# Gated stages of width 2816: three of four sums of weight blocks per pack by adding transfers, into doubled buffers

## The reference

```
def _swiglu(x, w_gate, w_up, w_down):
    return (jax.nn.silu(x @ w_gate) * (x @ w_up)) @ w_down
```

## Time and profile before

| | |
|---|---|
| time, median of 2 runs | 3442.8 us (3442.07 to 3443.53) |
| profiled execution, span from first to last instruction | 3441.6 us |
| TensorE busy | 3396.0 us, 99% of the span |
| VectorE busy | 2436.4 us, 71% |
| ScalarE busy | 1659.5 us, 48% |
| GpSimd busy | 133.9 us, 4% |
| TensorE clock granted, mean | 0.998 |
| DMA | 91 GB/s, 27% of the 16 engines' time in the SP queue |

### The profile page before, as it was taken

How to read it: one execution, slowest core, us unless ns; L and a number is a source line. 1 busy time by engine, 2 the same in 40 slices (tenths; PEclk the granted TensorE clock), 3 DMA queues, 4 the chain that set the end, 5 groups by cost and what they waited for, 6 DMA issues and landing times. The chain is left out here.

```text
span 3441.6 us, 63684 instructions
## 1 busy us (share of the span) xinstructions
PE 3396.0 (99%) x24351; PEld 3124.3 (91%) x24351; DVE 2436.4 (71%) x3572; ACT 1659.5 (48%) x2508; POOL 133.9 (4%) x129
## 2 busy tenths in 40 slices
PE   9999999999999999999999999999999999999998
PEld 8998899989998987887899889999999998799987
DVE  6886878877888655655888865657785367867863
ACT  4553655545554433333455545546555344455552
POOL 0100202000200100000002000000000000000000
PEclk9999999999999999999999999999999999999999
DMA  4333223332333322222223331212223321022232
GB/s 142 108 110 111 87 86 110 105 116 86 105 109 111 104 74 80 74 80 74 74 98 110 116 99 62 68 61 68 99 98 98 98 69 50 32 74 95 96 104 80
DMA packets 89618, 311.58 MB, mean 91 GB/s; under 512 B 10800, under 2 KB 15280, under 8 KB 89296
## 3 DMA queue, kind: packets, MB, share of 16 engines
q1 hardware_dynamic: 89056, 307.19, 26.9%
q0 software_dynamic: 368, 1.68, 0.2%
HBM read 306.73 MB, written 2.10 MB: 90 GB/s over the span
## 5 line engine op out<-in xcount | busy, mean ns | idle before, releaser
L821 PE MATMUL ps<-x_hi,w_hi 128*128 128x264 f32 (+2 forms) x2176 | 707.5, 325 | 2.6 <-ACT pair L2593 0.9
L821 PE MATMUL ps<-x_hi,w_lo 128*128 128x264 f32 (+2 forms) x2176 | 695.9, 320 | 0.0
L821 PE MATMUL ps<-x_lo,w_hi 128*128 128x264 f32 (+2 forms) x2176 | 694.1, 319 | 0.0
L2698 DVE TENSOR_TENSOR w_lo<-raw,w_hi 128x1024 fp32r<-128x1024 f32 x277 | 337.4, 1227 | 299.2 <-ACT w_hi L1685 296.8
L821 PEld LDWEIGHTS ps<-x_hi,w_hi 128*128 128x128 f32 x2176 | 410.1, 188 | 54.0 <-issue 17.8
L821 PEld LDWEIGHTS ps<-x_lo,w_hi 128*128 128x128 f32 x2176 | 409.6, 188 | 30.3
L821 PEld LDWEIGHTS ps<-x_hi,w_lo 128*128 128x128 f32 x2176 | 410.9, 189 | 28.6
L821 PE MATMUL ps<-h_hi,w_hi 128*128 128x264 f32 (+3 forms) x1296 | 410.7, 317 | 5.3 <-DVE h_lo L2905 1.9
L821 PE MATMUL ps<-h_hi,w_lo 128*128 128x264 f32 (+3 forms) x1296 | 399.6, 308 | 0.0
L821 PE MATMUL ps<-h_lo,w_hi 128*128 128x264 f32 (+3 forms) x1296 | 398.8, 308 | 0.0
L1685 ACT ACTIVATE w_hi<-raw 128x1024 fp32r<-128x1024 f32 x277 | 289.3, 1055 | 74.7 <-PE ps L821 50.6
(11 more groups left out here) (378 smaller groups left out, 7669.3 us busy)
## 6 DMA issues: line engine op xcount, KB each, us to landing
raw<-wstream SPq DMA_DIRECT2D x577, 512.0 KB, 3.3
res<-xT SPq DMA_DIRECT2D x8, 256.0 KB, 7.3
out<-res SPq DMA_DIRECT2D x8, 256.0 KB, 2.2
bias<-consts POOLq DMA_DIRECT2D x1, 1024.0 KB, 5.4
g_chunk<-consts POOLq DMA_DIRECT2D x1, 264.0 KB, 3.2
g_keep<-consts POOLq DMA_DIRECT2D x1, 256.0 KB, 3.3
par<-params SPq DMA_DIRECT2D x1, 232.5 KB, 7.7
ident<-consts SPq DMA_DIRECT2D x1, 64.0 KB, 6.4
```

The source lines that it names most:

```text
L821: m = pe.matmul(ps[:, bank, 0:n], w[:, slot, wt, :], x[:, k, c0:c0 + n], start=first and q == 0, stop=last and q == 2)
L2698: dve.tensor_tensor(w_lo[:, slot], raw[:, slot], w_hi[:, slot].bitcast(F32), ALU.subtract)\
```

## The change

The first three sums of a pack are no longer made on VectorE. GpSimd issues seven transfers of 256 KB per pack instead, each from the weights in HBM (`wstream`): three plain copies of B1 into three sum blocks, then two transfers that add B2 into two of them (`accum_op=ALU.add`), then two that add A1, to one of these and to the third block. The second kind waits for all three copies to have landed (M["copy"]), the third for the second (M["mid"]); the last two raise M["acc"]. VectorE keeps the fourth sum (`sum_4`), which waits for M["acc"], and ACT's step 1 waits for M["acc"] too. The sums of every second pack go to a second buffer, `m_sum1`, laid into columns of `x_hi` and `x_lo` (channels of the first half, tokens of the second half) that the packs don't read; its rows of 512 bytes are spaced by 528 floats. The transfers of pack m begin once the low parts of pack m - 2 are made (M["lo"] 2m - 2); those of the first pack of a stage wait for M["t"], those of the second for the end of the plain units (s_unit), which read the same columns of x. The scaling of `res` is moved: one instruction of 128x256 between the packs' transfers, from the third pack of a stage on, 16 in a stage.

```
+        m_sum1 = at("m_sum1", [P, 2, KD, T], offset=x_hi_at)
...
+        def made_block(up, s, b):
+
+            if up % 2:
+                return m_sum1[:, s, 0:KH, META + HALF + P * b:META + HALF + P * b + P]
+            return m_sum[:, 2 * s + b]
+
+        def made_pair(up, s):
+
+            if up % 2:
+                return m_sum1[:, s, 0:KH, META + HALF:T].rearrange("p k (b n) -> p b k n", b=2)
+            return m_sum[:, 2 * s:2 * s + 2]
+
+        def by_block(ap):
+
+            return ap.rearrange("p (b k) n -> p b k n", b=2)
...
                     if step in (0, 3):
                         load_of(u + step // 2 % 2, pack_slot(st, 2 * up + (step == 3)))
+                    elif step == 1:
+                        act.wait_ge(M["acc"], 32 * m + 32)
                     else:
-                        act.wait_ge(M["sum"], 3 * m + 3 - (step == 1))
+                        act.wait_ge(M["sum"], m + 1)
                     if first:
                         act.wait_ge(s_unit, st["u0"] + 4 + step + 1)
...
                     else:
-                        x = m_sum[:, 2:4] if step == 1 else m_sum[:, 0:2]
-                        act.activation(w_hi[:, slot], x.rearrange("p b k n -> p (b k) n"), ACT.Copy).then_inc(M["hi"], 1)
+                        act.activation(by_block(w_hi[:, slot]), made_pair(up, step % 2), ACT.Copy).then_inc(M["hi"], 1)
...
-                def sums_13(i, up):
+                def sum_4(i, up):
 
                     i, up = after(i, up)
-                    u = st["u0"] + 4 * i + 2 * up
-                    s = pack_slot(st, 2 * up)
-                    load_of(u, s)
-                    load_of(u + 1, s + 1)
-                    past(dve, M["lo"], 2 * pack_of(st, i, up))
-                    dve.tensor_tensor(made[:, 0:4:3], blocks[:, 2 * s:2 * s + 4:3],
-                                      blocks[:, 2 * s + 2:2 * s + 3].to_broadcast([P, 2, KH * P]), ALU.add)\
-                        .then_inc(M["sum"], 1)
-
-                def sum_2(i, up):
-
-                    i, up = after(i, up)
-                    m = pack_of(st, i, up)
-                    dve.wait_ge(M["sum"], 3 * m + 1)
-                    dve.tensor_tensor(made[:, 2], made[:, 3], blocks[:, 2 * pack_slot(st, 2 * up)], ALU.add)\
-                        .then_inc(M["sum"], 1)
-
-                def sum_4(i, up):
-
-                    i, up = after(i, up)
-                    m = pack_of(st, i, up)
-                    dve.wait_ge(M["sum"], 3 * m + 2)
-                    dve.tensor_tensor(made[:, 1], made[:, 2], blocks[:, 2 * pack_slot(st, 2 * up) + 1], ALU.add)\
-                        .then_inc(M["sum"], 1)
+                    m, u = pack_of(st, i, up), st["u0"] + 4 * i + 2 * up
+                    load_of(u, pack_slot(st, 2 * up))
+                    dve.wait_ge(M["acc"], 32 * m + 32)
+                    dve.tensor_tensor(made_block(up, 0, 1), made_block(up, 1, 0), raw[:, pack_slot(st, 2 * up), KH:KD],
+                                      ALU.add).then_inc(M["sum"], 1)
...
                 def packs(i, parts=(0, 1)):
                     for up in parts:
                         p, q, r = pack_banks(up)
-                        sums_13(i, up + 1)
+                        sum_4(i, up + 1)
                         add(i, up, 2, 1, r, 0, 0)
-                        sum_2(i, up + 1)
-                        sum_4(i, up + 1)
                         low(i, up + 1, 0)
                         add(i, up, 5, 3, p, 1, 1)
                         low(i, up + 1, 1)
...
+            def weight_sums(st, i, up):
+
+                m, u = pack_of(st, i, up), st["u0"] + 4 * i + 2 * up
+
+                def block(unit, half):
+                    return wstream[unit, :, KH * half:KH * half + KH]
+
+                if i == 2:
+                    pool.wait_ge(M["t"], 4 * st["r0"] + 4)
+                    if up:
+                        pool.wait_ge(s_unit, st["u0"] + 8)
+                else:
+                    pool.wait_ge(M["lo"], 2 * m - 2)
+                for b in range(2):
+                    pool.dma_start(made_block(up, 1, b), block(u + 1, 0)).then_inc(M["copy"], 16)
+                pool.dma_start(made_block(up, 0, 0), block(u + 1, 0)).then_inc(M["copy"], 16)
+                pool.wait_ge(M["copy"], 48 * m + 48)
+                for b in range(2):
+                    pool.dma_start(made_block(up, 1, b), block(u + 1, 1), accum_op=ALU.add).then_inc(M["mid"], 16)
+                pool.wait_ge(M["mid"], 32 * m + 32)
+                for b in range(2):
+                    pool.dma_start(made_block(up, b, 0), block(u, 0), accum_op=ALU.add).then_inc(M["acc"], 16)
+
+            def packs(st):
+
+                done = s_res if before(st)["kind"] == "load" else s_scale
+                for i in range(2, KF // 2):
+                    for up in range(2):
+                        weight_sums(st, i, up)
+                        if i > 2:
+                            r = res[:, i - 3, half_cols(S, up)]
+                            pool.tensor_scalar(r, r, ALPHA, None, ALU.mult).then_inc(done, 1)
+
...
                 b = before(st)
-                if st["kind"] == "glu":
-                    pool.wait_ge(M["t"], 4 * st["r0"] + 4)
-                    pool.wait_ge(M["mul"], 3 * quad_of(st, 5))
-                if b["kind"] == "load":
-                    for k in range(KD):
-                        pool.wait_ge(s_xlo, KD + k + 1)
-                        pool.tensor_scalar(res[:, k, META:T], res[:, k, META:T], ALPHA, None, ALU.mult)\
-                            .then_inc(s_res, 1)
-                    return
...
-                if n and (before(st)["kind"] == "load" or before(st).get("scaled")):
+                if st["kind"] == "glu":
+                    packs(st)
+                elif n and before(st).get("scaled"):
                     scale_residual(st)
```

More of the change, by code:

```diff
@@ L505, in build @@
         M = {name: sem("s_m_" + name) for name in (
-            "t", "thi", "tlo", "sum", "hi", "lo", "prod", "snap", "add", "silu", "mul")}
+            "t", "thi", "tlo", "copy", "mid", "acc", "sum", "hi", "lo", "prod", "snap", "add", "silu", "mul")}
         W = {name: sem("s_w_" + name) for name in (
@@ L1964, in project @@
                 if not st["n0"]:
-                    act.wait_ge(s_res, KD)
+                    act.wait_ge(s_res, 2 * KD)
                     act.wait_ge(s_eps, 1)
@@ L2723, in glu @@
                 last = KF // 2 - 1
-                blocks = raw[:, :, :, :].rearrange("p s (b k) n -> p (s b) (k n)", b=2)
-                made = m_sum[:, :, :, :].rearrange("p b k n -> p b (k n)")
                 def combine(c):
@@ L2809, in low @@
                         return
-                    x = m_sum[:, 2:4] if step == 1 else m_sum[:, 0:2]
-                    dve.tensor_tensor(w_lo[:, slot], x.rearrange("p b k n -> p (b k) n"), w_hi[:, slot].bitcast(F32),
+                    dve.tensor_tensor(by_block(w_lo[:, slot]), made_pair(up, step % 2), by_block(w_hi[:, slot]).bitcast(F32),
                                       ALU.subtract).then_inc(s_lo if step == 1 else M["lo"], 1)
@@ L2922, in glu @@
                 combined_low(3)
-                sums_13(2, 0)
-                sum_2(2, 0)
                 sum_4(2, 0)
@@ L3081, in project @@
                 if not st["n0"]:
-                    dve.wait_ge(s_res, KD)
+                    dve.wait_ge(s_res, 2 * KD)
                 else:
```

## The result

The changed kernel takes 4011.03 us (median of 2 runs, 4006.78 to 4015.27) against 3442.8 (3442.07 to 3443.53): ratio 1.165 [1.162, 1.168]. The direction and the mechanism came as forecast, but it cost 568 us where 188 were forecast, and the time lies above the range. The profiled execution has a span of 4012.9 us.

A forecast was written before the change was run, and what follows sets the result against it. TensorE was taken to bound the kernel (9.91 us per pack), then GpSimd's round. Per stage 9.6 + 1.3 + 2.4 + 33.6 = 46.9 us, four stages 188, giving 3631 us; range 3464 to 3880.

The forecast's parts named there:

- GpSimd's round sets the period: Packs 4 to 17 of each stage: GpSimd's 12.3 us against TensorE's 9.9, 2.4 us lost each, 33.6 per stage.
- R: GpSimd's own round per pack, without the last wave's landing: 12.3 us, 11.2 without a scaling, against TensorE's 9.91.
- wave of copies: First wave, GpSimd's three plain copies: 0.56 x 2 + 3.3 + 0.3 = 4.7 us until landed.
- second wave: Two transfers adding B2, taken as twice a copy's traffic: 2.8 us behind a fixed 2.6, 5.4 us.
- third wave, issue: GpSimd's issuing of the last two adding transfers, whose landing it doesn't wait for: 1.1 us.
- rival 1: Packs: chain hidden but for each stage's start, 3464 us, or 3502 with adding transfers as cheap as copies; chance 0.17.
- rival 2: Packs: adding transfers land after 7.3 us, each such wave 7.9, round 14.8, chain 20.5, 3811 us; chance 0.32 with worse.
- Pack 1's term: Its chain starts only with pack 0, so TensorE's product 7 of pack 0 comes at 18.1 instead of 8.5: 9.6 us lost.
- The engines' load: DMA engines per pack: 3.1 us of SP's loads plus 7.7 of the seven transfers, 10.8 us in a 9.91 us period.
- L: Latency of a pack's whole chain of three waves: 4.7 + 5.4 + 5.4 = 15.5 us.
- crowded row: Profile row of 256 KB transfers in a crowd at the program's start, 7.3 us, taken as an adding transfer's upper price.
- Rival 3: Stage starts: stalls lower TensorE's clock, four 10 us stalls adding 7 us; left in the range, no chance given.

The follow-up runs named there:

- experiment 1: Changed kernel with the four adding transfers of each pack made plain copies, same number, size, order and waits: 3718.9 us.
- experiment 6: Changed kernel with the scaling of res issued behind the stage's last transfers instead of between the packs: 3960.7 us.
- experiment 9: Changed kernel cut to two copies and two adding transfers per pack, VectorE making all sums of packs 0 and 1: 3522.56 us, ratio 1.023 to the kernel before.
- experiment 10: Changed kernel cut to one copy and one adding transfer per pack from pack 2 on, VectorE making all other sums: 3442.31 us, ratio 1.000.
- experiment 11: Separate program without the reference's work, only groups of transfers into both layouts, each waited for: two adding into whole rows 6.1 us, three copies 5.0 us.
- experiment 8: Changed kernel with GpSimd also waiting for the third wave to land before it scales and issues the next pack's copies: 4234.7 us.

## Why the prediction was wrong in size

**The model held.** "GpSimd's round sets the period": a wait-free succession of rounds, and experiments 1, 6, 9 and 10 move the time as the round does, down to no loss where it fits. From the landing to product 7 the prediction counted 2.6 us: 2.6. TensorE's loss is at product 7, VectorE's idle time is before sum 4 with a DMA as its releaser, the first packs are a term of their own, and the removed additions were worth 0 (experiment 10: 41 us of VectorE gone, ratio 1.000).

**The step that failed is the sizing of two waves in R.** For even packs, whose sums have whole rows (in brackets the odd ones, with rows of 512 bytes):

| term | predicted | measured |
|---|---|---|
| "wave of copies" | 4.7 | 7.3 (7.7) |
| "second wave" | 5.4 | 7.5 (8.7) |
| third wave, issue | 1.1 | 1.1 (1.5) |
| scaling | 1.1 | 0.8 |
| R | 12.3 | 16.8 (18.8), mean |

- *4.7 for the copies* left out that the third wave of the pack before is still in flight. The prediction said that R "lacks only the landing of the last wave". GpSimd does lack it, but the queue and the engines don't: the wait was removed from GpSimd and turned up in the next wave of copies, which takes 7.3 us where three copies alone take 5.0. SP's loads have no part in these 2.3 us, as none moved beside the copies.
- *5.4 for the second wave.* Counting twice the traffic was right for the engines: the trace's DMA packets of an adding transfer take 178 ns per 2048 bytes, 128 x 178 / 16 = 1.42 us of each engine against the 1.4 assumed, and a copy's 159 ns per 4096 bytes make 0.64 against 0.7. What failed is the step from engine time to the wave: alone such a pair takes 6.1, not 5.4. The second transfer is issued 0.57 us behind the first, a gap that the formulas of rivals 1 and 2 count and the forecast's sum leaves out; 5.4 + 0.57 = 6.0. The rest, 1.4 us, comes with SP's loads, both of which fall into this wave. The engines' share was used only to say that they would be overloaded; it was not put into the waves' latency. The rows from which the landing was priced had hardly a load beside them: 0.13 MB moved in q1 while the two transfers of 256 KB were in flight, although rival 1 says that they shared the engines with a load.
- *One price for both buffers.* The rows of 512 bytes, named under rival 2 as "four times as many pieces", were priced in no term. An adding packet of 512 bytes takes 65 ns: 2.1 us of each engine instead of 1.4. The odd rounds are 2.0 us longer than the even ones, some 14 us per stage over 7 of them. The adding is not all of it: with plain copies (experiment 1) they are 1.1 us longer.

**The first packs.** Pack 0 was to have 2.3 us to spare and is 2.6 us late: its chain takes from 35.0 to 55.73, 20.7 us instead of 15.5. Pack 1's term is 13.4 us on average against 9.6. The 16 periods behind it cost 126 us per stage against 37: there lies the miss.

**The engines' load** was put at 10.8 us per pack; 0.73 x 17.8 is 13.0. Both are above 9.91, which speaks against a version with shorter waits but all seven transfers keeping TensorE's pace; it was not tried. Experiment 10, with two transfers, has a share of 0.60.

**The range.** Rival 2 was near: it had the second wave at 7.9 and L at 20.5 (measured 7.5, and 20.7 for pack 0), but kept 4.7 for the copies, and so gave 3811. That its L came out is partly luck: pack 0's three waves take 8.8, 6.0 and 6.0 us, where it had 4.7, 7.9 and 7.9. The crowded row of 7.3 us would have fitted the copies as well: 1.1 + 7.3 = 8.4 in place of 4.7, R = 18.5, and the range would have reached past the measured time.

**Rival 1** (hidden but for the start) is excluded for seven transfers even with plain copies (experiment 1). **Rival 3**, the clock: the granted clock is 0.77 in the rounds shown above. After a wait the matmuls start some 0.21 us apart, and some 5 us later 0.12 us apart as before (in the timeline from 115.75, until 121.01): the granted clock is 0.50 from 116.5 to 120.8 us, the lower of TensorE's two levels (1.2 of 2.4 GHz), and 1.00 from 121.5 to 124.5. It is busy for 157.6 us more than before, and with its 414.7 us of waits at L933 that is 572, against 571.3 between the spans. But these 157.6 us are not a cause of their own: in the packs that wait TensorE stands for GpSimd's round anyway, and with a faster clock it would stand longer. The clock costs where no wait follows, in pack 17: 1.4 us in stage 1 and 6.3 in all four. The prediction had put 7 us on it, at the stages' starts.

## What to carry to other kernels

A chain of dependent transfers is priced wave by wave, each at its landing time under the load that the chain itself makes: with the last wave of the round before in flight, with the loads of the other queue beside it, and in its own row length. A wave that nobody waits for is not free: it is paid in the next one. And relief for an engine that has slack in the period is worth nothing, while the engine that takes the work over gets a period of its own, to be held against it first.

## What the hardware showed that I hadn't expected

- An adding transfer keeps small pieces: into rows of 512 bytes its packets are of 512 bytes (65 ns, 260 per 2 KB, against 178 for whole rows), while plain copies into the same rows go in packets of 4096 bytes, 159 ns in both layouts.
- A single 256 KB adding transfer lands 3.7 us after its issue with idle engines (4.6 into rows of 512 bytes), a copy 2.9 (3.5). In the packs of the kernel after, the median landing of the second wave is 6.2 us.
- GpSimd needs longer to issue one: the records show 0.88 us (whole rows) and 1.28 (rows of 512 bytes) against 0.54 to 0.58 for a copy into whole rows and 0.77 into rows of 512 bytes (experiment 11).
- Copies issued behind adding transfers of the same queue land 1.6 us later (5.1 against 3.5, experiment 8) though they write other blocks. Behind plain copies in flight they land after 3.7 (experiment 1).
